# Turning x for the first projections: from TensorE and a copy to VectorE straight into the pair buffers

## The reference

```python
h = (x @ w_in).astype(jnp.float32)        # layer 0: 1024 x 3088, split into q, k, v, g, lr
q, k, v, g, lr = jnp.split(h, [512, 1024, 2048, 3072], axis=-1)
...
h = x @ w_in                              # layer 1
u, z = jnp.split(h, [POOL_WIDTH], axis=-1)
...                                       # pooling is linear in u
m = jnp.einsum('btgc,gcd->btgd', p, w_grp) + b_grp
```

## Time and profile before

| | |
|---|---|
| median of 3 runs | 1883.43 us |
| the profiled execution's own time | 1884.62 us |
| its span, first to last instruction | 1882.9 us |
| mean granted TensorE clock | 0.992 of full speed |
| busy: PE, DVE, ACT, POOL | 1837.1, 1381.6, 842.8, 662.0 us |
| prepare / v steps / later steps of project | about 0 to 121 / 121 to 288 / 288 to 640 us |

### The profile page before, as it was taken

One profiled execution on the slowest core, in us unless ns is written; L12 is line 12 of the kernel. 1 busy time (PEld: TensorE's weight loads), 2 busy tenths in 40 slices (PEclk: granted clock), 3 DMA queues, 4 the chain that ended last, 5 costly groups with the idle time before them and its releaser, 6 DMA issues.

```text
span 1882.9 us, 24121 instructions
## 1 busy us (share of the span) xinstructions
PE 1837.1 (98%) x8514; PEld 1506.1 (80%) x8514; DVE 1381.6 (73%) x1666; ACT 842.8 (45%) x1294; POOL 662.0 (35%) x460
## 2 busy tenths in 40 slices
PE   9999999999999899999999999999999999999997
PEld 8878886887788788888678888878888887887885
DVE  3566565777566788787786768668899978447997
ACT  4554335556656534444444444454443344224231
POOL 0533233322231000235345655315576633223330
PEclk9999999999999899999999999999999999999999
DMA  9967664449354844676734444243456436637532
GB/s 307 323 211 249 215 208 166 125 109 281 91 142 129 293 162 160 209 249 199 269 106 140 151 148 143 90 157 123 157 187 205 154 121 229 240 140 268 179 146 101
DMA packets 278243, 342.81 MB, mean 182 GB/s; under 512 B 48368, under 2 KB 206832, under 8 KB 273520
## 3 DMA queue, kind: packets, MB, share of 16 engines
q1 hardware_dynamic: 275440, 333.98, 53.9%
q0 software_dynamic: 2688, 7.34, 1.2%
HBM read 221.73 MB, written 119.54 MB: 181 GB/s over the span
## 4 chain that ended last, share of the span: by engine, by line
PE 57%; DVE 5%; issue 2%; ACT 1%; DMA 1%; POOL 1%; DVEq 0%; ACTq 0%; POOLq 0%
PE banks L224 17%; PE banks L226 17%; PE banks L225 17%; PE banks L1755 1%; PE banks L1759 1%; DVE m_w_lo L2750 1%; DVE m_x_lo L2764 1%; PE banks L2533 1%; DMA m_ahead<-x_terms 1%; DVE a_w_lo L2004 0%; PE banks L1740 0%; PE banks L2493 0%; DVE a_stats L1981 0%; PE banks L1732 0%; DVE a_res L1978 0%
## 5 line engine op out<-in xcount | busy, mean ns | idle before, releaser
L224 PE MATMUL banks<-m_x_hi,m_w_hi 128*128 128x512 f32 x1312 | 514.9, 392 | 9.4 <-DVE m_z L2825 4.5
L226 PE MATMUL banks<-m_x_hi,m_w_lo 128*128 128x512 f32 x1312 | 513.4, 391 | 0.0
L225 PE MATMUL banks<-m_x_lo,m_w_hi 128*128 128x512 f32 x1312 | 512.9, 391 | 0.0
L224 PEld LDWEIGHTS banks<-m_x_hi,m_w_hi 128*128 128x128 f32 x1312 | 247.0, 188 | 65.9 <-issue 7.3
L225 PEld LDWEIGHTS banks<-m_x_lo,m_w_hi 128*128 128x128 f32 x1312 | 246.9, 188 | 53.2 <-issue 0.7
L226 PEld LDWEIGHTS banks<-m_x_hi,m_w_lo 128*128 128x128 f32 x1312 | 246.8, 188 | 52.4
L224 PE MATMUL banks<-b_hi,h_w_hi 128*128 128x512 f32 x656 | 256.7, 391 | 5.4 <-issue 3.4
L226 PE MATMUL banks<-b_hi,h_w_lo 128*128 128x512 f32 x656 | 255.6, 390 | 0.0
L225 PE MATMUL banks<-b_lo,h_w_hi 128*128 128x512 f32 x656 | 255.5, 389 | 0.0
L2557 ACT ACTIVATE m_w_hi<-m_s 128x512 fp32r<-128x512 f32 x182 | 114.4, 629 | 204.4 <-PE banks L226 176.9
L2750 DVE TENSOR_TENSOR m_w_lo<-m_s,m_w_hi 128x512 fp32r<-128x512 f32 x182 | 163.8, 904 | 32.6 <-ACT m_w_hi L2557 31.5
(11 more groups left out here) (274 smaller groups left out, 3363.2 us busy)
## 6 DMA issues: line engine op xcount, KB each, us to landing
b_raw<-x_in SPq DMA_DIRECT2D x14, 1024.0 KB, 9.7
m_x_raw<-x_terms SPq DMA_DIRECT2D x9, 1024.0 KB, 8.6
p_in<-in_pool_w_in SPq DMA_DIRECT2D x32, 256.0 KB, 5.2
w_fused<-p_out SPq DMA_DIRECT2D x32, 256.0 KB, 3.6
x_in<-h_terms SPq DMA_DIRECT2D x8, 1024.0 KB, 4.3
v_tiles<-h_v_out SPq DMA_DIRECT2D x16, 512.0 KB, 5.0
in_raw<-in_gla_w_in SPq DMA_DIRECT2D x16, 512.0 KB, 5.5
h_raw<-in_gla_w_in SPq DMA_DIRECT2D x16, 512.0 KB, 5.4
```

What stands on the lines that cost most here:

```text
L224: nc.tensor.matmul(out, a_hi, b_hi, start=first, stop=False, skip_group_check=True)
L225: nc.tensor.matmul(out, a_hi, b_lo, start=False, stop=False, skip_group_check=True)
L226: return nc.tensor.matmul(out, a_lo, b_hi, start=False, stop=last, skip_group_check=True)
```

## The change

VectorE turns x. It transposes 32 x 32 squares only, so the rows of x are loaded as four DMAs per tile with the squares placed such that one 128 x 1024 transpose gives a whole tile in a pair buffer, but with the contracted columns in another order: partition g * 32 + j, chunk k holds column g * 256 + k * 32 + j. So every weight that meets x must be loaded in that order (`by_rows`). The pair buffer is both what the step reads and what is stored to `x_in`; the loads back from `x_in` for the v steps are gone. Tiles 0 and 1 are turned in `prepare` (n = 16, 17), 2 and 3 at the start of `project`, tiles 2i + 4 and 2i + 5 at (i, 1) and (i, 3).

```diff
+    def load_x_rows(self, sp, u):
+        t = self.x_tile(u)
+        src = self.a["x"][0][t * P:(t + 1) * P, :].rearrange("(b i) c -> i b c", i=SQUARE)
+        for g in range(QUADS):
+            sp.dma_start(self.x_rows[u % 2][g * SQUARE:(g + 1) * SQUARE, :].rearrange("i (b c) -> i b c", b=QUADS),
+                         src[:, :, g * D // QUADS:(g + 1) * D // QUADS]).then_inc(self.x_rows_loaded[u % 2], DMA)
+    def turn_x(self, dve, u, raw):
+        dve.wait_ge(self.x_rows_loaded[u % 2], (u // 2 + 1) * QUADS * DMA)
+        out = raw[:, u % 2 * KT:(u % 2 + 1) * KT, :].rearrange("p k (b i) -> p b k i", i=SQUARE)
+        self.nc.vector.transpose(out, self.x_rows[u % 2][:].rearrange("p (b k j) -> p b k j", b=QUADS, j=SQUARE)
+                                 ).then_inc(self.x_turned, 1)
+    def store_x(self, sp, u, raw):
+        sp.wait_ge(self.x_turned, u + 1)
+        ...
+    def by_rows(self, w):
+        return w.rearrange("(g k j) c -> g j k c", g=QUADS, j=SQUARE)
# prepare
-    PAIR_AT = 23
+    TURNS_AT = {16: 0, 17: 1}
+    ROWS_AT = {9: 0, 10: 1, 18: 2, 19: 3}
-        v_src = a["gla_w_in"][0].rearrange("(k p) c -> p k c", p=P)
+        v_src = p.by_rows(a["gla_w_in"][0])
-                    sp.dma_start(p.b_raw[j][:, n, :], v_src[:, k + n, 2 * KD + c:2 * KD + c + BLK]
+                    sp.dma_start(p.b_raw[j][:, n, :], v_src[:, :, k + n, 2 * KD + c:2 * KD + c + BLK]
-                load_x(0)
...
-                    if x_tile(n) is not None and x_tile(n) + 1 < KT:
-                        load_x(x_tile(n) + 1)
-                    if x_tile(n) is not None and x_tile(n) >= 1:
-                        store_x(x_tile(n) - 1)
-                    if n == PAIR_AT:
-                        load_first_pair()
+                    if n in ROWS_AT:
+                        u = ROWS_AT[n]
+                        if u >= 2:
+                            p.store_x(sp, u - 2, p.in_raw0)
+                        p.load_x_rows(sp, u)
...
-                    if x_tile(n) is not None:                       # TensorE
-                        turn_x(x_tile(n))
-                    if x_tile(n) is not None:                       # ScalarE
-                        ...
-                        nc.scalar.activation(x_out[t % 2][:], x_ps[t % 2], ACT.Copy).then_inc(x_copied, 1)
+                    if n in TURNS_AT:                               # VectorE
+                        p.turn_x(dve, TURNS_AT[n], p.in_raw0)
# project, SyncE; the load of rank_raw goes from one DMA to four in the same way
                 for b in range(2):
-                    sp.dma_start(raws[i % 2][:, b * KT:(b + 1) * KT, :], w_src[:, :, column(i, b):column(i, b) + P]
-                                 ).then_inc(pair_loaded[i % 2], DMA)
+                    for g in range(QUADS):
+                        sp.dma_start(raws[i % 2][g * SQUARE:(g + 1) * SQUARE, b * KT:(b + 1) * KT, :],
+                                     w_src[g, :, :, column(i, b):column(i, b) + P]).then_inc(pair_loaded[i % 2], DMA)
-            load_rows(KT)
             last_store(sp)
-            load_pair(1)
             load_gk(0)
...
+            for u in (2, 3):
+                p.store_x(sp, u, raws[1])
+                p.load_x_rows(sp, u + 2)
-                    if n == 0 and i + 2 < STEPS:
+                    if n == 0 and V_STEPS <= i + 2 < STEPS:
...
+                    if i + 2 < V_STEPS and n in X_AT:                # X_AT = (1, 3)
+                        u = 2 * (i + 2) + X_AT.index(n)
+                        p.store_x(sp, u, raws[i % 2])
+                        if u + 2 < NT:
+                            p.load_x_rows(sp, u + 2)
# project, TensorE and ScalarE
-                    if i < HALF_K and n in (2, 5):
-                        turn_x(KT + 2 * i + n // 5)
-                    if i < HALF_K and n == 3:
-                        copy_x(KT + 2 * i)
-                    if 1 <= i <= HALF_K and n == -1:
-                        copy_x(KT + 2 * i - 1)
# project, VectorE; GpSimd and ScalarE wait for x_turned where they waited for the pair's load
+            turn_x(1, 0)
+            for n in range(PREPARED, HALF_K):
+                lo_part(0, n)
+            turn_x(1, 1)
+            for n in range(HALF_K, PRODUCTS):
                 lo_part(0, n)
             x_terms(0, 0)
             x_terms(0, 1)
...
+                    if n in X_AT and i + 2 < V_STEPS:
+                        turn_x(i + 2, X_AT.index(n))
```

More of the change, by code:

```diff
@@ L145, in __init__ @@
         assert self.at <= SBUF_END
+        self.at = self.w_end
+        self.x_rows = [self.place(f"x_rows{b}", [P, D]) for b in range(2)]
         self.mix_raw_at = self.rows_at - 2 * KT * P * 4
@@ L171, in x_tile @@
         return n // KT * KT + n % KT // 2 + n % 2 * HALF_K
[L173 to L178, removed]
+    def load_x_rows(self, sp, u):
[11 more added lines that the diff above has]
+        sp.wait_ge(self.x_turned, u + 1)
+        half, c, b = u // KT, u % KT // 2, u % 2
+        sp.dma_start(self.x_in[half, 2 * b:2 * b + 2, :, c, :].rearrange("q p n -> p q n"),
+                     raw[:, b * KT:(b + 1) * KT, :].rearrange("p (q k) t -> p q (k t)", q=2)
+                     ).then_inc(self.x_stored, DMA)
+    def by_rows(self, w):
+        return w.rearrange("(g k j) c -> g j k c", g=QUADS, j=SQUARE)
     def store_turned_keys(self, sp, first, head, src):
@@ L247, in prepare @@
     out = [p.place(f"p_out{s}", [P, GW]) for s in range(2)]
-    x_out = [p.place(f"p_x{s}", [P, KT, P]) for s in range(2)]
-    rows = [p.place(f"p_rows{s}", [P, D]) for s in range(ROWS)]
+    t_hi = [p.place(f"p_t_hi{s}", [P, GT, P], F32R) for s in range(2)]
+    t_lo = [p.place(f"p_t_lo{s}", [P, GT, P], F32R) for s in range(2)]
+    p.at = p.in_end + 9 * KT * P * 4
     grp_hi, grp_lo = [], []
@@ L253, in prepare @@
         grp_lo.append(p.place(f"p_grp_lo{s}", [P, GT, GW], F32R))
-    t_hi = [p.place(f"p_t_hi{s}", [P, GT, P], F32R) for s in range(2)]
-    t_lo = [p.place(f"p_t_lo{s}", [P, GT, P], F32R) for s in range(2)]
-    assert p.at <= SBUF_END
+    assert p.at <= p.w_end
     with ExitStack():
@@ L433, in turn @@
                     last.then_inc(turned, 1)
[L435 to L442, removed]
                 def warm(count):
@@ L512, in _ @@
                         else:
-                            act.wait_ge(p.in_loaded[0], 2 * DMA)
+                            act.wait_ge(p.x_turned, 1)
                         act.wait_ge(multiplied, (GROUPS - 1) * KT)
@@ L612, in project @@
     terms = p.place("h_terms", [P, 4, BLK])
-    p.at = g_at
-    rows = p.place("h_rows", [P, D])
-    x_out = p.place("h_x_out", [P, KT, P])
     p.at = p.qkv_end
@@ L772, in load_gk @@
                                  a["gla_w_gk"][0][:, h * DK:(h + 1) * DK]).then_inc(gk_loaded, DMA)
-            def load_rows(u):
-                if u > KT:
-                    sp.wait_ge(x_turned, u - KT)
-                first = p.x_tile(u) * P
-                sp.dma_start(rows[:], a["x"][0][first:first + P, :]).then_inc(rows_loaded, DMA)
-            def store_x(u):
-                sp.wait_ge(x_copied, u - KT + 1)
-                half, c, b = u // KT, u % KT // 2, u % 2
-                sp.dma_start(p.x_in[half, 2 * b:2 * b + 2, :, c, :].rearrange("q p n -> p q n"),
-                             x_out[:].rearrange("p (q k) t -> p q (k t)", q=2)).then_inc(x_stored, DMA)
             def store_x_terms(i):
@@ L1001, in turn_keys @@
                     last.then_inc(turned, 1)
-            def turn_x(u):
-                pe.wait_ge(rows_loaded, (u - KT + 1) * DMA)
-                if u > KT:
-                    pe.wait_ge(x_copied, u - KT)
-                for k in range(KT):
-                    last = nc.tensor.transpose(p.ps[:, 6 + k // HALF_K, k % HALF_K * P:(k % HALF_K + 1) * P],
-                                               rows[:, k * P:(k + 1) * P], p.ident[:])
-                last.then_inc(x_turned, 1)
             for i in range(STEPS):
@@ L1048, in gates_free @@
                     if m < HEADS:
-                        act.wait_ge(x_stored, KT * DMA)
+                        act.wait_ge(p.x_turned, NT)
                 elif m:
@@ L1331, in x_terms @@
                 if part == 0:
-                    dve.wait_ge(pair_loaded[i % 2], 2 * (i // 2 + 1) * DMA)
+                    dve.wait_ge(*pair_ready(i))
                     dve.wait_ge(terms_stored, i * DMA)
@@ L1437, in norm_of, with turn_x @@
                                             ALU.mult).then_inc(normed, 1)
-            for n in range(PREPARED, PRODUCTS):
+            def turn_x(i, b):
+                o = i - 2
+                if o >= 0:
+                    dve.wait_ge(w_hi_done, PRODUCTS * (o + 1))
+                    dve.wait_ge(w_lo_done, parts_to(o, PRODUCTS - 1))
+                    dve.wait_ge(x_summed, 4 * (o + 1))
+                    dve.wait_ge(p.x_stored, 2 * (o + 1) * DMA)
+                    if o:
+                        dve.wait_ge(w_summed, 4 * o)
```

(3 more changed lines are left out.)

81 lines of the change are left out of this document (22 added, 59 removed).

## The result

The changed kernel takes **1903.74 us** (median of 4 runs, 1903.01 to 1904.38); the kernel before takes 1883.83 us beside it. The ratio is 1.0106 [1.0093, 1.0118]: 20 us slower, where 1883.9 was forecast and the range ended at 1897.0. The profiled execution of the changed kernel took 1904.38 us, 19.8 more than that of the kernel before.

A forecast was written before the change was run, and what follows sets the result against it. TensorE, busy 98% of the span, was taken as the bound. Terms: -17.7 taken off, +3.0 head, +2.5 pairs, +12.7 value loads, together +0.5 us on 1883.43: 1883.9 us, no change; range 1868.5 to 1897.

The forecast's parts named there:

- the value-load term: Prepare: value loads beginning with 4 use only four DMA engines, so TensorE waits 12.7 us; ends 0 and 32.7.
- Rival (c): Prepare's value loads: the four engines give only prepare's mean rate, 20.1 GB/s each; +20.5 us, 1904; chance 0.06.
- the head: Head of project: two turns first, GpSimd beside VectorE and late rows make TensorE wait 3.0 us; ends 0 and 6.
- the v steps: Steps 0 to 3: without two tiles of x each, they take 8.0 us less.
- Taken off in prepare: Prepare: transposes of x leave TensorE, 6.8 us, and three waits of 2.9 us go; 9.7 us saved.
- Transposes of 128 x 1024: VectorE's turns of x: one takes 1.4 us, between 0.71 and 1.42.
- Rival (d): V steps: they don't get shorter, turns beside GpSimd slow to 3.7 us and `add_u3` comes late; +8.5, 1892; chance 0.05.
- The weight pairs: Ends of steps 7 and 15: eight DMAs for a pair instead of two cost 2.5 us; ends 0 and 27.
- Rival (b): Pairs 9 and 17: their eight DMAs hold SyncE ahead of the moving side; +12.6 us, 1896; chance 0.09.
- Rival (a): Prepare's value loads: spread over the DMA engines as before, so no cost; -12.2 us, 1871.2; chance 0.28.

The follow-up runs named there:

- the kernel by halves: Changed kernel with each value load as two DMAs of 64 partitions, source pattern beginning with 2; 1945.25 us, ratio 1.0321 to the kernel before.
- the kernel by quarters: Changed kernel with each value load filling 32 partitions with four 2 KB runs, source pattern beginning with 32; 1883.15 us, ratio 0.9988 to the kernel before.
- the run with two loads: Changed kernel, values loaded by quarters, weight pairs as two DMAs in the old row order instead of eight; 1877.82 us, ratio 0.9969 to the kernel before.
- with `x` stored first: Changed kernel, values by quarters, x's tiles 2 and 3 stored and rows of 4 and 5 loaded ahead of the gates' weights; 1879.95 us, ratio 0.9978.

## Why the prediction was wrong

**The step that failed is the size of the value-load term.** Its mechanism, four engines for loads whose pattern begins with 4, is what the runs show; its size was taken as 12.7 us, and it measures 27.7: the first seed of the changed kernel, 144.85, less that of the same kernel with the old loads, 117.15. The new loads alone move the first seed of the kernel before by 24.5 us (148.94 less 124.43).

The rate was the wrong row. I divided 1770 kB by the 26.0 GB/s of the window from 284 to 296 us; by the prediction's own working the loads took 51.4 + 4.0 + 27.7 = 83.1 us, or 21.3 GB/s for an engine. The packets say about the same without that working: while exactly four were in flight, the changed kernel moved 87.4 GB/s, 21.9 for an engine, and the kernel by halves, with two, 23.3 for an engine. The prediction had a nearer row beside it, prepare's own 321 GB/s at a share of 1.00, 20.1 for an engine, and gave it only to the rival of 1904 us with a chance of 0.06.

Rival (c) named the time, +20.5 where 20.0 was measured, but that it is so close is partly luck. Its 32.7 us for the loads make +23.0 to the first seed, 2.6 more than measured; the head, the v steps and the pairs came out 2.1 us worse than forecast and cancel most of it. Nor is a share of 1.00 a fixed rate: it goes with 416 and 321 GB/s, and in the kernel by quarters with 264 at 1.02. The rate depends on which transfers run.

The Trainium skill (DMA: Bandwidth & Descriptors, "Why a DMA increments its semaphore by 16 and not by 1") gives the number of engines as the largest up to 16 that divides the slowest dimension of both patterns. The runs agree: 264, 202 and 146 GB/s for 32, 4 and 2, and four and two packets in flight. The rate that the Trainium skill gives (same page, "Where 436 GB/s comes from"), with which the term was an estimate of 9.6 us, is further off than the trace's.

**Taken off in prepare**, 9.7 us: right in kind and a little low, 11.6 without waits for transfers. Turns 3.2 us apart from 109.61 on, and the waits for `p_t_lo` gone. With the old value loads 7.3 of it are seen (117.15 for 124.43); the loads of prepare leave no more.

**The v steps**, 8.0, and **the head**, 3.0: together -5.0 forecast, -3.8 measured. Steps 1 to 3 take 1.85 us less each, as the rows said. Step 0 takes 1.73 us more where some 0.5 was due. The wait is 2.1 us where 3.0 was forecast, and the lower clock behind it adds about 1.6. The way there was seen rightly: VectorE's operations beside GpSimd take 1.77 us, and the rows land late. What I left out is that a wait of TensorE can cost more than its length.

**Transposes of 128 x 1024**: 1.24 us, 1.4 taken. Rival (d) falls, since the steps behind step 0 last 19.04 us. Whether GpSimd slows such a transpose isn't shown: none of the sixteen ran beside one of its sums, but for 0.18 us of one in prepare.

**The weight pairs**, 2.5 us: 3.4 by the ledger, 4.7 by the run with two loads (24.91 - 24.17, 23.27 - 19.84 and 21.47 - 20.42, less 0.5 given back between). At step 7 I let 1.4 us pass through, and 0.7 did, of 4 us more in the queue; at step 15 I counted a third of 3.1, and 3.4 passed. The 0.7 is less than that place moves without any change of the pairs (2.4 us, above). That a place has a wait does not tell how much slack the one beside it has. Rival (b) falls: eight took 6.80 and 4.22 us, not over 15.

**Rival (a)**, the values spread as before, falls with the result and with the packets. Its sum can be held against the changed kernel with the old loads: 1871.2 against 1877.93. By the seeds of the profiled executions that kernel gains 5.1 us where 12.2 were summed, and of the 7.1 between them 2.4 lie in prepare (7.3 for 9.7), 1.8 in the head and the v steps (3.2 for 5.0) and 2.9 in the pairs (5.4 for 2.5).

**The range** had its upper end at 1897 although the text worked out 1904 from a row. The bound was kept in the term and left out of the range.

Open: why a DMA into 32 partitions of four runs is slower than one into 128 partitions of one; what the eight loads of a pair cost at the first turn; and which transfer ends the few waits that are left in prepare of the version by quarters.

## What to carry to other kernels

When a load is rewritten for another row order, look at what its pattern begins with on both sides: with 4 or 2 entries there no more engines than that carried it, and in a stretch where DMA is the limit this cost every transfer beside it. Splitting the same load along that dimension gave back 20.6 us (1903.74 less 1883.15), and with `x` stored first the change is 4 us faster than the kernel before (ratio 0.9978 [0.9969, 0.9987]). To price a transfer, take the rate of the same stretch before that of a faster window with other transfers, treat it as a bound (here 20.1 and 26.0 GB/s for an engine lay on either side of the 21.9 measured), and keep such a bound in the range.

## What was not expected of the hardware

- Behind waits of 2.6 to 3.5 us TensorE ran one tile at 1.2 GHz, the four transposes in 1.11 us instead of 0.60. At two of the three places in prepare this cost nothing (first seed 144.78 for 144.85 with the clock back in the window of 90 to 115 us). At the head of project it cost about 1.6 us behind a wait of 2.1 us; behind waits of 1.7 and 1.9 us at the same place the clock stayed at 1.00.
- The mean DMA share falls when the deal is uneven (0.68 with four engines, 0.48 with two, 1.02 with all), while each transfer takes longer (with four, `p_in` 9.9 us to landing instead of 5.2). The mean hides the busy four: in the changed kernel fewer than four packets were in flight for only 1.0 of 51 us.
- A DMA of 256 KB into 32 partitions with four runs in each, in place of one into 128 partitions, cost 4 us over sixteen loads in prepare, whichever rows it read.
